# Memory heads of a two-block transformer kernel: the scores and transposes of two steps issued together, their dense products in one piece, and a semaphore of its own for narrow score blocks

## The reference

```python
def memory_attn(q, mk, mv):
    s = jnp.einsum('bshd,bmhd->bhsm', q, mk).astype(jnp.float32) * (dm ** -0.5)
    p = jax.nn.softmax(s, axis=-1).astype(mv.dtype)
    return jnp.einsum('bhsm,bmhd->bshd', p, mv).reshape(B, S, Hm * dm)

# in each of the two layers of the second block
y = jnp.concatenate([..., memory_attn(qm, mk, mv)], axis=-1) * jax.nn.silu(gate)
x = x + y @ w_out
```

## Time and profile before

| | |
|---|---|
| median of the runs | 1918.35 us (1917.21 to 1919.05) |
| the profiled execution's own time | 1917.82 us |
| its span, first to last instruction | 1916.1 us |
| TensorE busy (matmul) | 1893.5 us, 99% |
| VectorE busy | 1068.7 us, 56% |
| ScalarE busy | 786.9 us, 41% |
| GpSimd busy | 163.5 us, 9% |
| mean granted TensorE clock | 0.997 of full speed |
| first memory segment, main loop | about 1424 to 1462 us |
| second memory segment, main loop | about 1797 to 1834 us |

### The profile page before, as it was taken

How to read it: one execution, slowest core, us unless ns; L and a number is a source line. 1 busy time by engine, 2 the same in 40 slices (tenths; PEclk the granted TensorE clock), 3 DMA queues, 4 the chain that set the end, 5 groups by cost and what they waited for, 6 DMA issues and landing times.

```text
span 1916.1 us, 25428 instructions
## 1 busy us (share of the span) xinstructions
PE 1893.5 (99%) x9090; PEld 1512.7 (79%) x9090; DVE 1068.7 (56%) x1711; ACT 786.9 (41%) x1256; POOL 163.5 (9%) x241
## 2 busy tenths in 40 slices
PE   9999999999999999999999999999999999999997
PEld 7888888888888777688888888866677887777776
DVE  7787534434456667644343446476666555555553
ACT  6576422222234444532312234355554343444442
POOL 3111000000000000000000000000002053531000
PEclk9999999999999999999999999999999999999998
DMA  7323232323322122222322232111313232322221
GB/s 250 113 94 121 99 96 91 114 83 99 101 96 77 56 66 66 79 90 97 109 99 88 92 108 85 67 45 61 94 56 93 81 94 80 90 76 92 74 97 61
DMA packets 49854, 173.83 MB, mean 91 GB/s; under 512 B 7472, under 2 KB 9648, under 8 KB 49776
## 3 DMA queue, kind: packets, MB, share of 16 engines
q1 hardware_dynamic: 43312, 162.62, 25.4%
q0 software_dynamic: 6464, 10.19, 2.2%
HBM read 168.58 MB, written 4.21 MB: 90 GB/s over the span
## 4 chain that ended last, share of the span: by engine, by line
PE 94%; DVE 2%; ACT 2%; issue 1%; DMA 1%; DVEq 0%; SPq 0%; ACTq 0%
PE ps L477 17%; PE ps L479 17%; PE ps L478 17%; PE sc L477 5%; PE sc L479 5%; PE sc L478 5%; PE tr L479 4%; PE tr L477 4%; PE tr L478 4%; PE ps L647 3%; PE tr L613 3%; PE sc L587 2%; PE ps L587 2%; PE sc L618 1%; PE ps L634 1%
## 5 line engine op out<-in xcount | busy, mean ns | idle before, releaser
L994 ACT ACTIVATE Wh<-Wr 128x1024 fp32r<-128x1024 f32 (+2 forms) x268 | 300.3, 1121 | 648.3 <-PE ps L479 294.7
L477 PE MATMUL ps<-Hh,Wh 128*128 128x512 f32 x1136 | 465.8, 410 | 0.0
L479 PE MATMUL ps<-Hh,Wl 128*128 128x512 f32 x1136 | 444.3, 391 | 0.0
L478 PE MATMUL ps<-Hl,Wh 128*128 128x512 f32 x1136 | 443.2, 390 | 0.0
L1427 DVE TENSOR_TENSOR Wl<-Wr,Wh 128x1024 fp32r<-128x1024 f32 (+2 forms) x268 | 352.4, 1315 | 132.4 <-ACT Wh L994 131.1
L477 PEld LDWEIGHTS ps<-Hh,Wh 128*128 128x128 f32 x1136 | 213.5, 188 | 56.3 <-issue 16.4
L479 PEld LDWEIGHTS ps<-Hh,Wl 128*128 128x128 f32 x1136 | 213.2, 188 | 46.9
L478 PEld LDWEIGHTS ps<-Hl,Wh 128*128 128x128 f32 x1136 | 213.9, 188 | 39.4 <-issue 0.5
L477 PE MATMUL sc<-Hh,Wh 128*128 128x512 f32 x432 | 168.9, 391 | 0.0
L479 PE MATMUL sc<-Hh,Wl 128*128 128x512 f32 x432 | 168.2, 389 | 0.0
L478 PE MATMUL sc<-Hl,Wh 128*128 128x512 f32 x432 | 168.1, 389 | 0.0
(11 more groups left out here) (289 smaller groups left out, 2556.8 us busy)
## 6 DMA issues: line engine op xcount, KB each, us to landing
Wr<-in_w SPq DMA_DIRECT2D x228, 512.0 KB, 3.5
Wr<-in_w SPq DMA_DIRECT2D x32, 768.0 KB, 4.4
Wr<-in_w SPq DMA_DIRECT2D x16, 640.0 KB, 3.9
scr<-in_rpb POOLq DMA_DIRECT2D x128, 24.0 KB, 2.2
X<-in_x SPq DMA_DIRECT2D x8, 256.0 KB, 3.9
Wr<-in_wri SPq DMA_DIRECT2D x4, 512.0 KB, 3.4
out_t<-X SPq DMA_DIRECT2D x8, 256.0 KB, 2.3
scr<-d_rel POOLq DMA_DIRECT2D x8, 192.0 KB, 3.8
```

What stands on the lines that cost most here:

```text
L477: pe.matmul(bank[:, 0:n], hi, rh[:, k, :], start=(k == 0), stop=False)
L478: pe.matmul(bank[:, 0:n], hi, rl[:, k, :], start=False, stop=False)
L479: return pe.matmul(bank[:, 0:n], lo, rh[:, k, :], start=False, stop=(k == kc - 1))
L994: act.activation(place(Wh, slot, kc), place(Wr, slot, kc), ACT.Copy).then_inc(w_hi, 1)
```

## The change

On TensorE the loop of `mem_heads` now goes by two steps. One turn of it, for an even j, issues the scores of g and g+1, then `values` where it is due, then the transposes of g-2 and g-1, then the four k steps (12 matmuls) that belonged to both. In the second segment the very first pump (j = 0) still stands ahead of the first scores. VectorE's and ScalarE's `mem_heads` are as they were.

In `scores` the wide heads signal `t_s` by 2 each, the second narrow matmul signals `nb_ok` and no longer `t_s`, and the readers of a narrow block wait for `nb_ok`, with counts worked out anew. GpSimd's load of the second memory segment waits for `nb_ok` too.

```diff
@@ load_mem (GpSimd)
                 pool.wait_ge(t_s, STEP0[seg])
+                if seg == "mem1":
+                    pool.wait_ge(nb_ok, 80)
@@ scores (TensorE)
                         if c1 == k1:
-                            mm.then_inc(t_s, 1)
+                            mm.then_inc(t_s, 1 if kind == GQA else 2)
                 if kind != GQA:
                     pe.wait_ge(nb_ok, narrow)
-                    head(t + 1, 1, *span(t + 1)).then_inc(t_s, 2)
+                    head(t + 1, 1, *span(t + 1)).then_inc(nb_ok, 1)
@@ mem_heads (TensorE)
-                    for j in range(8):
+                    for j in range(0, 8, 2):
...
-                        mem_scores(g, i, j, ring[2 * i + j // 4] if early else (QT, KT2)[i][:, j // 4, :])
-                        if i or j or early:
-                            pump(j, 2, UNIT0[name] + q, TAKEN0[name] + q, q % 2)
-                        if g - 2 >= g0:
-                            mem_turn(g - 2, (j - 2) % 8)
+                        queries = ring[2 * i + j // 4] if early else (QT, KT2)[i][:, j // 4, :]
+                        for x in range(2):
+                            mem_scores(g + x, i, j + x, queries)
                         if j in (2, 6) and g - 3 >= g0:
                             hd = 2 * i + (j - 6) // 4
                             values(g - 3, hd // 2, hd % 2, OUT0[seg] + hd)
+                        if g - 2 >= g0:
+                            for x in range(2):
+                                mem_turn(g - 2 + x, (j - 2 + x) % 8)
+                        for x in range(0 if i or j or early else 1, 2):
+                            pump(j + x, 2, UNIT0[name] + q, TAKEN0[name] + q, q % 2)
@@ exps (ScalarE)
                 if kind == STICK:
-                    act.wait_ge(t_s, g + 2)
+                    if t % 2:
+                        act.wait_ge(nb_ok, narrow)
+                    else:
+                        act.wait_ge(t_s, g + 4)
@@ before_exp (VectorE)
-                dve.wait_ge(t_s, g + 2)
+                if kind != GQA and t % 2:
+                    dve.wait_ge(nb_ok, narrow)
+                else:
+                    dve.wait_ge(t_s, g + (2 if kind == GQA else 4))
```

More of the change, by code:

```diff
@@ L774, in pair @@
                             scores(kind, g, par, t, first=first and t == 0,
-                                   narrow=2 * i + (t // 2 + (1 if kind == STICK else 25)))
+                                   narrow=4 * i + (2 * (t // 2) + (1 if kind == STICK else 49)))
                         pumped(2 * t)
@@ L945, in _ @@
                         scores(kind, g, i % 2, t, (i % 4) // 2, first=i % 4 == 0 and t == 0, queries=ring[i % 4],
-                               narrow=2 * (i - 4) + t // 2 + 17)
+                               narrow=4 * (i - 4) + 2 * (t // 2) + 33)
                     pump(2 * t, 2, ub + first, tb + first, first % 2)
@@ L1066, in ffn, with exps @@
                 out_proj(f"down{layer}b", norm)
-            def exps(kind, g, t, i=0):
+            def exps(kind, g, t, i=0, narrow=None):
                 w = P * len(key_chunks(kind, block_of(kind, t)))
                 if kind == STICK:
-                    act.wait_ge(t_s, g + 2)
+                    if t % 2:
+                        act.wait_ge(nb_ok, narrow)
+                    else:
+                        act.wait_ge(t_s, g + 4)
                     wait(act, t_p, g - 2)
@@ L1278, in pair @@
                         g = 8 * i + (g0 + 2 * t)
-                        exps(kind, g, t)
+                        exps(kind, g, t, narrow=4 * i + (2 * (t // 2) + 2))
                         pumped(2 * t)
@@ L1542, in ffn, with before_exp @@
                 out_proj(f"down{layer}b", nrm)
-            def before_exp(kind, g, t, i=0, par=0, between=None):
+            def before_exp(kind, g, t, i=0, par=0, between=None, narrow=None):
                 b = block_of(kind, t)
@@ L1879, in pair @@
                             first_low = lambda: split(nu * i + (ub + 4), 1 - (nu * par + 3) % 2, KD)
-                        before_exp(kind, g, t, 0, par, first_low)
+                        before_exp(kind, g, t, 0, par, first_low, 4 * i + (2 * (t // 2) + 50))
                         pumped(2 * t)
@@ L2046, in _ @@
                         expand(i + 2)
-                    before_exp(kind, g, t, i - 4)
+                    before_exp(kind, g, t, i - 4, narrow=4 * (i - 4) + 2 * (t // 2) + 34)
                     if i == 0 and t == 0:
```

## The result

| | before | after |
|---|---|---|
| median of 7 runs each | 1918.35 us (1917.04 to 1919.05) | 1925.57 us (1925.40 to 1926.08) |
| ratio | | 1.004 (1.003 to 1.005) |
| the profiled execution's own time | 1917.82 us | 1925.79 us |
| its span | 1916.1 us | 1924.1 us |

The kernel became 7.2 us slower. The forecast was 1927.0, within 1923.0 to 1931.0. In the changed kernel all lines of the memory heads have moved: the scores are line 620 (618 before), the transposes 627 (625), `values` 636 (634), the exponential 1112 (1104), the maximum 1620 (1609), the releasing multiplication 1629 (1618) and the readout of a gate unit 1828 (1817). Dense products are lines 479 to 481.

A forecast was written before the change was run, and what follows sets the result against it. TensorE was taken to bound the kernel, so its new waits are paid in full: 5.34 + 1.93 + 1.77 - 0.3 = +8.7 us on 1918.35 gives 1927.0 us, own range 1924.5 to 1930.5, wider range 1923.0 to 1931.0.

The forecast's parts named there:

- six ordinary waits: Three turns per segment following a unit's readout: transposes wait for VectorE's multiplication of g-1, 0.89 us each, 5.34 in all.
- first wait, first segment: Turn i = 0, j = 2: transposes wait for step 1's multiplication, behind a weight's subtraction on VectorE, 1.93 us.
- first wait, second segment: Same turn, with one pump ahead of the first scores: transposes wait for VectorE's multiplication, 1.77 us.
- dense pace, fewer changes of kind: 192 dense matmuls in the memory segments run at an uninterrupted unit's pace: 0.3 us gained, bounds 0 and 0.7.
- semaphores: New signals on score blocks: TensorE's matmuls, order and reader releases unchanged, so 0 us, bounds 0.5 either way.
- What bounds the kernel: TensorE is busy 99% of the span, so its waits are paid in full unless a later wait absorbs them.
- The turns with `values`: Three turns per segment: `values`, 1.72 us, covers the second transposes, so no wait; without that cover 0.7 us each.
- The second chain: Rival, 11 in 100: scores wait for ScalarE's exponential behind a weight copy, or turns with `values` wait; the latter gives 1931.
- Changes between kinds of matmul: Rival, 3 in 100: 16 dense/float32 changes removed in the segments save more, 1916.3 us; 0.56 us each decides the sign.
- the Trainium skill's failure mode: Rival, 2 in 100: small pauses between matmul groups lower TensorE's clock in the stages with waits, +22 us, 1949.
- The 216 ns: Skill's full-clock pace at 512 columns; reached in pieces of 12, an estimated 2.7 us back; left out of the sum.

The follow-up runs named there:

- e4: Changed kernel with VectorE doing both maxima, then both normalizations of a pair, and ScalarE's weight copy behind the pair's second exponential: 1915.43 us, ratio 0.9992.
- e10: Kernel before, old semaphores kept, with the memory heads on TensorE, VectorE and ScalarE all working by pairs: 1917.76 us, ratio 1.0001.
- e6: Changed kernel with the memory `values` matmuls behind the transposes instead of ahead of them: 1930.96 us, ratio 1.0069.
- e5: Changed kernel with 6 of the 12 dense matmuls moved between the paired scores and the paired transposes: 1919.64 us, ratio 1.0011.
- e7: Changed kernel with VectorE's readout of a gate unit behind the next step's maximum and normalization: 1927.18 us, ratio 1.0049.
- e1: Changed kernel with TensorE's memory-head loop as before, leaving only the semaphore part: 1916.32 us, ratio 0.9993.
- e2: Kernel before with the paired TensorE loop and the old semaphores: 1926.26 us, ratio 1.0047.

## Why the prediction was right

The sum, term by term, with what the runs showed:

| term | forecast | measured |
|---|---|---|
| six ordinary waits | 5.34 (0.89 each) | 5.6 (0.93 each, turns of the changed kernel against e4) |
| first wait, first segment | 1.93 | 1.94 |
| first wait, second segment | 1.77 | 1.85 |
| dense pace, fewer changes of kind | -0.3 (0 to -0.7) | -0.54 (segments of e4 and e10 against before) |
| semaphores | 0 (+-0.5) | -1.5 in the score groups (24 of 0.0625), of which -0.8 reached the stages |
| sum | +8.7 | +7.4, or +8.1 with the -0.8; profiled executions +8.0, medians +7.2 |

That +7.4 lies so near to the medians' +7.2 is partly luck. The segments are 8.9 us longer, the stages with narrow groups 0.8 shorter, and the two profiled executions differ by 8.0. The medians of the kernel before went from 1917.44 to 1918.35 us between the sets of runs, so their difference can't choose between 7.4 and 8.1.

- *What bounds the kernel.* Right: TensorE's idle time appeared in the segments and nothing took it up again.
- *The ordinary waits.* Right in place, number and cause. Two errors in their size nearly cancel. The maximum started at 0.81 us and not 0.86, so the wait itself is 1.92 - 1.08 = 0.84. But the turn is longer than that: from the transposes' start to the next scores it takes 3.04 us in the first segment (1435.28 to 1438.32) and 3.06 in the second (1811.19 to 1814.25), where an unbroken order needs 4.04 - 1.08 = 2.96. A wait costs some 0.1 us more than its length here, and e6's 0.72 to 0.76 for an expected 0.67 says the same.
- *The first waits.* Their chain stayed where it was, to 0.02 us (6.65 for 6.63, and 5.09 for 5.09). ScalarE's share showed as the wait of scores 3, as said.
- *The turns with `values`.* Right: no wait, and e6 gives the price without the cover, 0.72 to 0.76 for the 0.7 that was named.
- *The pairing's gain.* Inside its bounds, and nearer to the upper one than I took it.
- *The semaphore part.* **This step failed.** It said that nothing moves on TensorE, since the matmuls, their order and the waits are the same, and it bounded the cost only by how late a reader could be. But in 40 groups a wait of its own went out of TensorE's stream, and in 24 of them the next dense matmul came 0.0625 us sooner for it. What the form of a signal does to that matmul's own start was not among the things I priced. It gave 1.5 us in the score groups, three times the bound, and 0.8 of it in the stages of the changed kernel.
- *The rivals.* The second chain did not show in the changed kernel beyond scores 3; it showed in e5 and e7, where the cover was shifted. Changes between kinds of matmul and the dense pace together are worth 0.54 us in 16, far from the 0.56 each that would have turned the sign. The clock stayed at 1.00 in both segments, so the Trainium skill's failure mode (TensorE: Matmul & The Clock Gate, A second HAM failure mode: psum-queue depth-cycling) did not appear with waits of up to 1.1 us. The 216 ns that the Trainium skill gives for a matmul of 512 columns (the same page, Back-to-back issue gap) was not reached in pieces of 12 either: they kept 0.23 us.

The best kernel run here is e4: 1915.43 us, 0.9992 (0.9983 to 1.0001) of the kernel before, so below what this measurement can tell from it in total. Its two gains are seen in the stages alone.

## What to carry to other kernels

When work on one engine is regrouped, its partner's order has to be regrouped with it. An instruction that waits for "step g-1 done" really waits for everything its partner has queued ahead of that, and here that included the scores just issued. So work out, per wait, how much work of the waiting engine stands between the trigger and the wait, and compare it with the partner's chain (here 1.92 us against 1.08, and with `values` 2.80). And where a matmul both waits and signals, look in the trace whether its wait has become an instruction of its own. Here that cost 0.06 us a group, and it was gone in each form in which the matmul signalled by 1 a semaphore that its neighbour does not signal.

## What the runs showed that I had not expected

- The second narrow matmul of a score group (float32, 64 rows) loads its weights 0.06 us later, 0.81 and not 0.75 us after the group's start, when its wait for `nb_ok` is an instruction of its own. It was one wherever the matmul signalled `t_s` by 2, and not where it signalled `nb_ok` or a third semaphore by 1. Which of the two, the semaphore or the step, decides it is open.
- The stick-breaking heads have the same pair of blocks, and their score matmuls take the same time in both forms (9.25 us between 700 and 780 us in the kernel before, e1 and e2). Their load moves as well, from 0.82 us after the group's first load (646.61 to 647.43) to 0.76 in e1 (646.18 to 646.94). The next matmul starts 0.97 us after the group's first in both, behind the wide heads' matmuls, so the gain is hidden there.
- An ordinary wait of TensorE cost about 0.09 us beyond its length here (3.04 to 3.06 us against 2.96 from the transposes to the next scores).
- The sum of a wait and its cover can be right and the time still miss, where the shifted work stands in a third engine's queue: e5 and e7 both lost on ScalarE what they had won against VectorE.
